# A planned two-stream layer kernel: the order of ScalarE and VectorE by latest times in place of recorded order

## The chip, the cores and the metric

One Trainium2 chip, all 8 cores, no exchange between them. The metric is the device time of the slowest core in microseconds. Engines are named as in the profile: PE is TensorE (matmuls), PEld its weight loads, DVE is VectorE, ACT is ScalarE, POOL is GpSimd and SP is SyncE.

## What is computed

Two layers over x of shape (4, 4096, 1024). Cut to what matters:

```python
for i in range(2):
    h = rmsnorm(x, pre_mix_g)
    proj = h @ w_in + b_in                       # 1024 -> 5120: z, u, v, two gates
    ya = pool_mixer(z) @ w_pa                    # trailing means over 2, 4, 8, 16 positions
    yb = (gelu(u) * (tril(w_s) @ layernorm(gelu(v)) + b_s)) @ w_pb    # in chunks of 128
    x = x + rmsnorm((sigmoid(ga) * ya + sigmoid(gb) * yb) @ w_o, post_mix_g)
    x = x + rmsnorm(square(relu(rmsnorm(x, pre_ffn_g) @ w_ff1)) @ w_ff2, post_ffn_g)
    x = x + rmsnorm(sigmoid(x @ w_ple_gate) * (p[i] @ w_ple_proj), post_ple_g)
```

## The kernel before

Each core owns 2048 positions (and 128 ahead of them as a halo), with the channels on the partitions. The positions are four tiles of 512, worked in two pairs: stream A holds tiles 0 and 2, stream B tiles 1 and 3. Names that end in A or B belong to a stream (XA is its residual, U0A to U56A are its bf16 working tiles, RBA its norm factors). For each pair of tiles and each layer, TensorE runs a group of one to three weight blocks first for A and then for B, so that the weights are loaded once for two tiles (WB has four buffers of one block). Tile 0 has 16 or 32 more columns than the others and so takes two of the eight PSUM banks for each product where the others take one.

The order of a stage, for A and then for B: u (gelu, L740 with tile U3), half of z (L644), v (gelu, L709, its statistics L712), half of the first gate (sigmoid, L740 with U4); then `v_norm` (Ln and Exp, L1080) and the normalised v of both streams (L728, Identity, one for each 128 positions: eight, or nine with the halo); then the rest of z, the gates, the spatial gating product (L788 on TensorE, read by L769 and L772 on VectorE), the pool map, w_pa, w_pb (L844 multiplies by the gate, L847 adds ya), w_o (L859 squares, L863 or L867 scaled copy), ff1 (L931 relu to TMP, L933 product), ff2, and the last stage with the sigmoid gate (L1005 to TMP), the projection (L1015) and their product (L1021), of which ScalarE makes squares (L1024). A sum over channels is a product with ones on TensorE (L500), followed by Ln (L508) and Exp (L511); the residual that follows is eight or twelve operations on VectorE (L891, then L896 or L901), and ScalarE converts its result for the next product (L906, L910).
The pool chain of one chunk: L642 copies the last 16 columns of the tile before into a slot, L644 evicts z behind them, and one to four adds (L659) and L664 follow, through S1 and S2, which both streams share. B has three slots for four chunks.

Nothing is issued as it is written. Each operation is recorded with an engine, a planned duration (for a ScalarE operation from PSUM with a pointer 136 + 0.833 n + 93 ns for n columns, for VectorE from SBUF 185 + 1.042 n) and the operations that it depends on by its tiles. Those dependences are fixed by the recorded order. `Prog._schedule` then simulates the five engines: TensorE, GpSimd and SyncE take their operations in recorded order; ScalarE and VectorE take, whenever they are free, among the operations that are ready the one with the smallest key. The key is `nominal`, the TensorE time recorded ahead of the operation (`late` is 0 everywhere), plus 2500 ns where it needs another table than the one loaded; and such an operation may start only `HOLD_NS` after the last one that used the loaded table. DMAs go through one lane in that simulation: 12 us for the first load of XB (L430), 6.6 us for a weight block. The order that comes out is written to the engines, with a semaphore wait for each dependence.

Of the kernel before, what the change touches and what calls it, by code (L numbers as in the profile page):

```python
# [30 lines left out]
SEM_NS = 90.0  # L31
TABLE_NS = 1300.0
HOLD_NS = 400.0
NS_COL = 0.417

# [8 lines left out]

class Op:
    __slots__ = ("i", "eng", "fns", "ns", "deps", "sem", "inc", "table", "nominal", "late", "tok", "users",
                 "left", "ready", "end")

    def __init__(self, i, eng, fns, ns, deps, sem, inc, table, nominal, late):  # L50
        self.i, self.eng, self.fns, self.ns, self.deps = i, eng, fns, ns, deps
        self.sem, self.inc, self.table, self.nominal, self.late = sem, inc, table, nominal, late
        self.tok = None
        self.users = []
        self.left = 0
        self.ready = 0.0
        self.end = 0.0

class Prog:  # L60
# [6 lines left out]
    def __init__(self):  # L67
        self.ops = []
        self.semh = {}
        self.clock = 0.0  # L70
        self.q = {k: [] for k in self.ENG}

    def add_sem(self, key, handle):
# [29 lines left out]
    def dma(self, eng, sem, fn, ns, reads=(), writes=()):  # L103
        return self._record(eng, [fn], ns, reads, writes, sem, 16)

    def _schedule(self):
        order = {k: [] for k in self.ENG}
        queue = {k: [] for k in self.ENG}
        for o in self.ops:
            o.users = []  # L110
        for o in self.ops:
            o.left = len(o.deps)
            o.ready = 0.0
            for d in o.deps:
                d.users.append(o)
            if o.eng not in self.FREE:
                queue[o.eng].append(o)
        head = {k: 0 for k in self.ENG}
        free = {k: 0.0 for k in self.ENG}
        table, table_end = None, 0.0  # L120
        dma_free = 0.0
        pools = {k: [o for o in self.ops if o.eng == k and o.left == 0] for k in self.FREE}
        left = len(self.ops)
        while left:
            best = None
            for k in self.ENG:
                if k in self.FREE:
                    ps = pools[k]
                    if not ps:
                        continue  # L130
                    def may(o):
                        if o.table is None or o.table == table:
                            return o.ready
                        return max(o.ready, table_end + HOLD_NS)
                    t = max(free[k], min(may(o) for o in ps))
                    pick, key = None, None
                    for o in ps:
                        if may(o) > t:
                            continue
                        x = o.nominal + o.late  # L140
                        if o.table is not None and o.table != table:
                            x += 2500.0
                        if key is None or (x, o.i) < key:
                            pick, key = o, (x, o.i)
                    o = pick
                else:
                    if head[k] >= len(queue[k]):
                        continue
                    o = queue[k][head[k]]
                    if o.left:  # L150
                        continue
                    t = max(free[k], o.ready)
                if best is None or t < best[0]:
                    best = (t, o)
            assert best is not None, "the recorded order cannot run"
            t, o = best
            k = o.eng
            order[k].append(o)
            left -= 1
            if k in self.FREE:  # L160
                pools[k].remove(o)
                dur = o.ns
                if o.table is not None and o.table != table:
                    dur += TABLE_NS
                    table = o.table
                free[k] = o.end = t + dur
                if o.table is not None:
                    table_end = o.end
            elif k == "pe":
                head[k] += 1  # L170
                free[k] = o.end = t + o.ns
            else:
                head[k] += 1
                free[k] = t + 100.0
                dma_free = max(t + 1500.0, dma_free) + o.ns
                o.end = dma_free + 500.0
            for u in o.users:
                u.left -= 1
                u.ready = max(u.ready, o.end + SEM_NS)
                if u.left == 0 and u.eng in self.FREE:  # L180
                    pools[u.eng].append(u)
        self.span = max(o.end for o in self.ops)
        return order

    def build(self, final_eng, final):
# [45 lines left out]
def build_nc():  # L231
# [11 lines left out]
    with ExitStack() as es:  # L243
# [252 lines left out]
        def tail_ones(sq, rsq, cbl):  # L496

            bks = banks(len(cbl))
            for dc in range(8):
                fns = [lambda e, bk=bk, dc=dc, c0=c0, w=w: e.matmul(  # L500
                    PS[:, bk, 0:w], ONEB[:], sq(dc, c0, c0 + w), start=(dc == 0), stop=(dc == 7))
                    for bk, (c0, w) in zip(bks, cbl)]
                P.group(fns, sum(w for _, w in cbl) * NS_COL, reads=[rOne] + rsq(dc), writes=[rPS[bk] for bk in bks])
            return bks
# [771 lines left out]
```

How the kernel before makes its waits and increments, by code:

```python
    def build(self, final_eng, final):  # L185
        order = self._schedule()
        cnt = {}
        for k in self.ENG:
            for o in order[k]:
                cnt[o.sem] = cnt.get(o.sem, 0) + o.inc
                o.tok = (o.sem, cnt[o.sem])
        for k in self.ENG:
            seen = {}
            q = self.q[k]
            for o in order[k]:
                self._waits(k, o.deps, seen, q)
                q.extend(o.fns[:-1])
                s = self.semh[o.sem]
                q.append(lambda e, fn=o.fns[-1], s=s, n=o.inc: fn(e).then_inc(s, n))
            if k == final_eng:
                self._waits(k, final, seen, q)
# [1 line left out]
    def _waits(self, k, deps, seen, q):  # L203
        need = {}
        for d in deps:
            key, val = d.tok
            if key == "pe" and k == "pe":
                continue
            if seen.get(key, 0) >= val:
                continue
            if need.get(key, 0) < val:
                need[key] = val
        for key, val in need.items():
            seen[key] = val
            s = self.semh[key]
            q.append(lambda e, s=s, val=val: e.wait_ge(s, val))
```

## Time and profile before

| | us |
|---|---|
| three runs | 2300.98, 2302.17, 2674.32 (median 2302.17) |
| the profiled execution, its device time | 2302.23 |
| its span, slowest core (core 2) | 2300.7 |
| spans of the eight cores | 2287.4 to 2300.7 |

How to read the rows further on: a busy share says how long an engine ran something; a row of waits says for how long an engine stood still and which operation let it go on (engine, tile, line); a timeline row has start, duration, engine, line, operation, out<-in with shapes and count, and in brackets the idle time before it with its releaser. A row of windows has the bounds and length, then the busy us and instructions of PE, PEld, DVE, ACT and POOL, TensorE's granted clock as a share of full speed, the share of the DMA engines and GB/s.

### The profile page before, as it was taken

To read this page: it belongs to the slowest core of one execution; us is meant where nothing else is said; L and a number is where in the kernel's file an instruction comes from. 1 tells how busy PE (TensorE), PEld (TensorE's weight loads), DVE (VectorE), ACT (ScalarE), POOL (GpSimd) and SP (SyncE) were. 2 spreads that over 40 slices of the span, in tenths; PEclk is the share of its full clock that TensorE was granted. 3 is DMA by queue.
4 is the path that set the end of the run, shared out by engine and by line. 5 is a ranking of instruction groups with operands and counts; after the bars stand their busy time and mean duration, and the time that the engine had idled before them with its cause. 6 is when DMAs were issued, how large, how long until landed. Compare 5 with 4: busy or idle time off the path is not lost.

```text
span 2300.7 us, 30001 instructions; the slowest of 8 cores (2287.4 to 2300.7 us)
## 1 busy us (share of the span) xinstructions
PE 2116.7 (92%) x10640; PEld 1053.2 (46%) x10818; DVE 1019.7 (44%) x1607; ACT 855.7 (37%) x1344; POOL 82.2 (4%) x156
## 2 busy tenths in 40 slices
PE   2989979999798999999979999999989989999995
PEld 1546646666444444444434444444434444444442
DVE  2427553402662755420454565541165375543035
ACT  2353063312645306321454522531165441543134
POOL 0000000000000000000000000000000000000000
PEclk8999989999999999999989999999999999999998
DMA  8332534434343253445484343354343434335331
GB/s 178 56 56 47 92 56 65 75 57 82 72 69 60 47 92 55 68 89 91 84 216 96 65 80 63 66 95 74 55 83 57 76 61 78 69 65 92 62 58 74
DMA packets 36326, 176.83 MB, mean 77 GB/s; under 512 B 3282, under 2 KB 6482, under 8 KB 18770
## 3 DMA queue, kind: packets, MB, share of 16 engines
q0 software_dynamic: 22912, 148.92, 38.1%
q1 hardware_dynamic: 13268, 25.98, 3.5%
q8 instruction: 90, 1.47, 0.3%
q14 instruction: 56, 0.46, 0.1%
HBM read 315.40 MB, written 8.39 MB: 141 GB/s over the span
## 4 chain that ended last, share of the span: by engine, by line
PE 83%; DVE 5%; ACT 5%; issue 5%; DMA 2%; DVEq 0%; SPq 0%; ACTq 0%
PE PS L583 71%; PE PS L701 5%; PE PS L500 3%; DMA XB<-xT 2%; PE PS L805 1%; PE PS L705 1%; DVE XB L896 1%; PE PS L788 1%; ACT U2A L728 1%; DVE XA L901 1%; PE PS L1015 0%; DVE XA L896 0%; ACT U0B L906 0%; ACT L508 0%; ACT TMP L1005 0%
## 5 line engine op out<-in xcount | busy, mean ns | idle before, releaser
L583 PE MATMUL PS<-U0A,WB 128*128 128x512 bf16 (+2 forms) x2907 | 531.7, 341 | 78.5 <-ACT U3A L740 23.5
L583 PE MATMUL PS<-U0B,WB 128*128 128x512 bf16 x2252 | 508.0, 381 | 3.8 <-DVE T L668 1.1
L583 PEld LDWEIGHTS PS<-U0A,WB 128*128 128x128 bf16 x2944 | 291.7, 100 | 302.0 <-issue 88.9
L583 PEld LDWEIGHTS PS<-U0B,WB 128*128 128x128 bf16 x2304 | 225.0, 98 | 268.1 <-issue 7.8
L931 ACT ACTIVATE TMP<-PS 128x512 f32<-128x512 f32 (+1 forms) x256 | 150.3, 597 | 265.4 <-PE PS L583 259.3
L859 ACT ACTIVATE U1A<-PS 128x512 bf16<-128x512 f32 (+1 forms) x64 | 37.5, 605 | 391.2 <-PE PS L583 391.2
L394 POOL DMA_DIRECT2D WB<-wst x144 | 76.3, 531 | 2142.0 <-PE PS L583 1637.4
L583 PE MATMUL PS<-U56B,WB 128*128 128x512 bf16 x504 | 128.1, 406 | 14.5 <-DVE U56B L847 14.1
L583 PE MATMUL PS<-U2B,WB 128*128 128x512 bf16 x498 | 123.7, 395 | 16.1 <-ACT TMP L1005 15.4
L583 PE MATMUL PS<-U2A,WB 128*128 128x512 bf16 (+1 forms) x631 | 123.8, 343 | 10.1 <-ACT TMP L1005 9.7
L583 PE MATMUL PS<-U3A,WB 128*128 128x512 bf16 (+1 forms) x637 | 118.1, 338 | 0.2
L583 PE MATMUL PS<-U3B,WB 128*128 128x512 bf16 x504 | 117.1, 379 | 0.4
L583 PE MATMUL PS<-U56A,WB 128*128 128x512 bf16 (+1 forms) x628 | 116.4, 337 | 0.6
L859 ACT ACTIVATE U1B<-PS 128x512 bf16<-128x512 f32 x64 | 37.4, 598 | 172.1 <-PE PS L583 171.9
L583 PEld LDWEIGHTS PS<-U2A,WB 128*128 128x128 bf16 x640 | 62.7, 99 | 63.9 <-issue 16.3
L583 PEld LDWEIGHTS PS<-U56B,WB 128*128 128x128 bf16 x512 | 52.6, 103 | 84.1 <-issue 31.1
L583 PEld LDWEIGHTS PS<-U2B,WB 128*128 128x128 bf16 x512 | 51.3, 101 | 81.3 <-issue 27.6
L583 PEld LDWEIGHTS PS<-U3A,WB 128*128 128x128 bf16 x640 | 62.7, 98 | 49.2
L583 PEld LDWEIGHTS PS<-U56A,WB 128*128 128x128 bf16 x640 | 62.6, 98 | 49.1
L583 PEld LDWEIGHTS PS<-U3B,WB 128*128 128x128 bf16 x512 | 50.1, 98 | 59.8
L659 DVE TENSOR_TENSOR S<-S 128x525 f32<-128x525 f32 (+5 forms) x96 | 67.4, 702 | 2.9
L769 DVE SCALAR_TENSOR_TENSOR TMP<-PS,CPACK,BF 128x512 f32<-128x512 f32 (+1 forms) x72 | 49.2, 691 | 36.1 <-PE PS L788 32.2
(184 smaller groups left out, 2243.4 us busy)
## 6 DMA issues: line engine op xcount, KB each, us to landing
WB<-wst POOLq DMA_DIRECT2D x136, 1024.0 KB, 8.7
XB<-xT SPq DMA_DIRECT2D x2, 2048.0 KB, 26.5
WB<-wst POOLq DMA_DIRECT2D x8, 512.0 KB, 5.4
outT<-XA SPq DMA_DIRECT2D x16, 256.0 KB, 3.9
outT<-XB SPq DMA_DIRECT2D x16, 256.0 KB, 2.2
XA<-xT SPq DMA_DIRECT2D x4, 528.0 KB, 9.4
U2A<-wsT SPq DMA_DIRECT2D x4, 512.0 KB, 4.0
BF<-bsbc SPq DMA_DIRECT2D x4, 512.0 KB, 4.8
```

Of the source, the lines that this page charges most:

```text
L394: lambda e: e.dma_start(out=WB[:, b, 0:n], in_=wst[l, j, :, 0:n]), 1.6 * n, reads=list(behind), writes=[rW[b]])
L500: fns = [lambda e, bk=bk, dc=dc, c0=c0, w=w: e.matmul(PS[:, bk, 0:w], ONEB[:], sq(dc, c0, c0 + w), start=(dc == 0), stop=(dc == 7)) for bk ...
L583: return lambda e: e.matmul(PS[:, bk, 0:w], WB[:, b, k * kstride + fi * 128: k * kstride + (fi + 1) * 128], rhs(k, c0, c0 + w), start=(k = ...
L659: P.op("dve", dve_ns(COLS - lo, False), lambda e, nxt=nxt, cur=cur, co=co, d=d, lo=lo: e.tensor_tensor(out=nxt[:, lo:COLS], in0=cur[:, lo ...
L701: fns = [lambda e, k=k, lhs=lhs, b=b, bk=bk: e.matmul(PS[:, bk, :], lhs[k], WB[:, b, k * 512:(k + 1) * 512], start=(k == 0), stop=False) f ...
L705: fns.append(lambda e, bk=bk, v0=v0: e.matmul(PS[:, bk, :], ONEB[0:2, :], VB2[0:2, v0:v0 + 512], start=False, stop=True))
L728: P.op("act", act_ns(1024, False, 2), lambda e, c=c, src=src, dst=dst: e.activation(out=dst, in_=src, func=AF.Identity, scale=S.RSTD[:, c ...
L769: P.op("dve", dve_ns(n, True), lambda e: e.scalar_tensor_tensor(out=out, in0=in0, scalar=cv(l, V_LNG, h), in1=in1, op0=ALU.mult, op1=ALU.add),
L788: fns = [lambda e, c=c: e.matmul(PS[:, bk, c * 128:(c + 1) * 128], S.flat(2, c * 2048 + h * 256, 128, BF16), WSB[:, h * 128:(h + 1) * 128] ...
L805: fns.append(lambda e, bk=bk, o0=o0, g=g, cc=cc, c0=c0, w=w: e.matmul(PS[:, bk, 0:w], WB[:, b4, o0:o0 + 128], S.u(1, 2 * g + cc, c0, c0 + ...
L859: P.op("act", act_ns(self.n, True), lambda e: e.activation(out=sv(self.sq(oc, a, b), self.cbs), in_=ps(bks, self.cbs), func=AF.Square), re ...
L931: P.op("act", act_ns(self.n, True), lambda e: e.activation(out=sv(t, self.cbs), in_=ps(bks, self.cbs), func=AF.Relu), reads=rp, writes=[rT ...
```

## The change

The key of ScalarE's and VectorE's operations becomes `due`, a latest time counted backward from the end. The planner simulates forward, computes latest times, and simulates again, eight times in all: the first round uses the old key, the second the times of `_latest` (no engine but TensorE is limited), the later ones those of `_backward`, which runs the same simulation from the end to the start with one operation at a time on each engine and, among those possible, the one that ended last in the forward simulation. The round with the shortest planned span is emitted. Besides, a dependence between two TensorE groups is no longer charged 90 ns, and the 2500 ns have a name.

```diff
--- before.py
+++ after.py
@@ -31,6 +31,8 @@
 SEM_NS = 90.0
 TABLE_NS = 1300.0
 HOLD_NS = 400.0
+SWITCH_NS = 2500.0
+ROUNDS = 8
 NS_COL = 0.417
 
 
@@ -45,7 +47,7 @@
 
 class Op:
     __slots__ = ("i", "eng", "fns", "ns", "deps", "sem", "inc", "table", "nominal", "late", "tok", "users",
-                 "left", "ready", "end")
+                 "left", "ready", "end", "due")
 
     def __init__(self, i, eng, fns, ns, deps, sem, inc, table, nominal, late):
         self.i, self.eng, self.fns, self.ns, self.deps = i, eng, fns, ns, deps
@@ -55,6 +57,7 @@
         self.left = 0
         self.ready = 0.0
         self.end = 0.0
+        self.due = 0.0
 
 
 class Prog:
@@ -68,6 +71,7 @@
         self.ops = []
         self.semh = {}
         self.clock = 0.0
+        self.spans = []
         self.q = {k: [] for k in self.ENG}
 
     def add_sem(self, key, handle):
@@ -103,16 +107,102 @@
     def dma(self, eng, sem, fn, ns, reads=(), writes=()):
         return self._record(eng, [fn], ns, reads, writes, sem, 16)
 
+    def _links(self):
+        for o in self.ops:
+            o.users = []
+        for o in self.ops:
+            for d in o.deps:
+                d.users.append(o)
+
+    def _latest(self):
+
+        last = {k: None for k in self.ENG}
+        for o in reversed(self.ops):
+            t = 0.0
+            for u in o.users:
+                t = min(t, u.due - (0.0 if o.eng == u.eng == "pe" else SEM_NS))
+            if o.eng not in self.FREE:
+                nx = last[o.eng]
+                if nx is not None and o.eng == "pe":
+                    t = min(t, nx.due)
+                last[o.eng] = o
+            o.due = t - (o.ns if o.eng in ("pe",) + self.FREE else o.ns + 2000.0)
+
+    def _backward(self):
+
+        left = {}
+        ready = {}
+        users = {}
+        for o in self.ops:
+            left[o] = len(o.users)
+            ready[o] = 0.0
+        nxt = {k: [o for o in reversed(self.ops) if o.eng == k] for k in self.ENG}
+        head = {k: 0 for k in self.ENG}
+        free = {k: 0.0 for k in self.ENG}
+        pools = {k: [o for o in self.ops if o.eng == k and left[o] == 0] for k in self.FREE}
+        n = len(self.ops)
+        while n:
+            best = None
+            for k in self.ENG:
+                if k in self.FREE:
+                    ps = pools[k]
+                    if not ps:
+                        continue
+                    t = max(free[k], min(ready[o] for o in ps))
+                    o = max((o for o in ps if ready[o] <= t), key=lambda o: (o.end, o.i))
+                else:
+                    if head[k] >= len(nxt[k]):
+                        continue
+                    o = nxt[k][head[k]]
+                    if left[o]:
+                        continue
+                    t = max(free[k], ready[o])
+                if best is None or t < best[0]:
+                    best = (t, o)
+            t, o = best
+            k = o.eng
+            n -= 1
+            if k in self.FREE:
+                pools[k].remove(o)
+                e = free[k] = t + o.ns
+            elif k == "pe":
+                head[k] += 1
+                e = free[k] = t + o.ns
+            else:
+                head[k] += 1
+                free[k] = t + 100.0
+                e = t + o.ns + 2000.0
+            o.due = -e
+            for d in o.deps:
+                left[d] -= 1
+                ready[d] = max(ready[d], e + (0.0 if k == d.eng == "pe" else SEM_NS))
+                if left[d] == 0 and d.eng in self.FREE:
+                    pools[d.eng].append(d)
+
     def _schedule(self):
+        self._links()
+        best = None
+        for o in self.ops:
+            o.due = o.nominal + o.late
+        for n in range(ROUNDS):
+            order = self._forward()
+            if best is None or self.span < best[0]:
+                best = (self.span, order, {o: o.end for o in self.ops})
+            if n % 2 == 0 and n < 2:
+                self._latest()
+            else:
+                self._backward()
+        self.span, order, ends = best
+        for o, e in ends.items():
+            o.end = e
+        return order
+
+    def _forward(self):
         order = {k: [] for k in self.ENG}
         queue = {k: [] for k in self.ENG}
         for o in self.ops:
-            o.users = []
-        for o in self.ops:
             o.left = len(o.deps)
             o.ready = 0.0
-            for d in o.deps:
-                d.users.append(o)
             if o.eng not in self.FREE:
                 queue[o.eng].append(o)
         head = {k: 0 for k in self.ENG}
@@ -121,6 +211,12 @@
         dma_free = 0.0
         pools = {k: [o for o in self.ops if o.eng == k and o.left == 0] for k in self.FREE}
         left = len(self.ops)
+
+        def may(o):
+            if o.table is None or o.table == table:
+                return o.ready
+            return max(o.ready, table_end + HOLD_NS)
+
         while left:
             best = None
             for k in self.ENG:
@@ -128,18 +224,14 @@
                     ps = pools[k]
                     if not ps:
                         continue
-                    def may(o):
-                        if o.table is None or o.table == table:
-                            return o.ready
-                        return max(o.ready, table_end + HOLD_NS)
                     t = max(free[k], min(may(o) for o in ps))
                     pick, key = None, None
                     for o in ps:
                         if may(o) > t:
                             continue
-                        x = o.nominal + o.late
+                        x = o.due
                         if o.table is not None and o.table != table:
-                            x += 2500.0
+                            x += SWITCH_NS
                         if key is None or (x, o.i) < key:
                             pick, key = o, (x, o.i)
                     o = pick
@@ -176,10 +268,11 @@
                 o.end = dma_free + 500.0
             for u in o.users:
                 u.left -= 1
-                u.ready = max(u.ready, o.end + SEM_NS)
+                u.ready = max(u.ready, o.end + (0.0 if k == u.eng == "pe" else SEM_NS))
                 if u.left == 0 and u.eng in self.FREE:
                     pools[u.eng].append(u)
         self.span = max(o.end for o in self.ops)
+        self.spans.append(round(self.span / 1000, 1))
         return order
 
     def build(self, final_eng, final):
```

## Rows read from the trace of the kernel before

**Rows 1.** The page: busy time by engine; the chain that ended last.
```profile
PE 2116.7 (92%) x10640; PEld 1053.2 (46%) x10818; DVE 1019.7 (44%) x1607; ACT 855.7 (37%) x1344; POOL 82.2 (4%) x156
...
PE 83%; DVE 5%; ACT 5%; issue 5%; DMA 2%; DVEq 0%; SPq 0%; ACTq 0%
```

**Rows 2.** TensorE's waits: total us, times, longest us.
```profile
PE PS L583 <- ACT TMP L1005: 25.0, 10, 7.1
PE PS L583 <- ACT U3A L740: 23.5, 3, 20.3
PE PS L583 <- ACT U4B L740: 18.4, 4, 7.8
PE PS L583 <- DVE U56B L847: 14.1, 4, 3.7
PE PS L1015 <- ACT TMP L1005: 13.1, 10, 2.8
PE PS L583 <- DVE U2A L933: 12.8, 4, 9.0
PE PS L583 <- DVE U0A L553: 12.7, 4, 4.3
...
PE PS L788 <- ACT U56B L644: 10.7, 3, 4.6
...
PE PS L1015 <- DVE U3A L1021: 3.2, 1, 3.2
```

**Rows 3.** Windows by engine; before the last two columns the clock.
```profile
365.00:575.00 210.00, 209.27 (x1371) 135.31 (x1383) 54.24 (x72) 52.54 (x87) 9.88 (x18) 1.00 0.46 76
886.00:893.00 7.00, 6.10 (x15) 2.25 (x16) 2.59 (x5) 4.73 (x10) 0.53 (x1) 0.51 0.19 19
...
sum 111.00, PE 77.08 PEld 32.63 DVE 57.64 ACT 72.64 POOL 2.12; mean PE 4.82 PEld 2.04 DVE 3.60 ACT 4.54 POOL 0.13
```

**Rows 4.** Timeline, ScalarE and TensorE, 1283 to 1304: start, us, what.
```profile
1283.25 1.24 ACT L728 ACTIVATE U2A<-U56A,NMR,RSTD 128x1024 bf16<-128x1024 f32 x1 [0.44 <-DVE NMR L1085]
...
1292.43 1.28 ACT L740 ACT_TABLE_LOAD   x1
1293.72 2.42 ACT L740 ACTIVATE U4B<-PS,CPACK 128x512 bf16<-128x512 f32 x4
...
1303.18 0.39 PE L788 MATMUL PS<-WSB,U2A 128*128 128x128 bf16 x4
```

**Rows 5.** Timeline, VectorE and ScalarE, 1296 to 1331 us.
```profile
1296.82 0.71 DVE L659 TENSOR_TENSOR S<-U56A 128x527 f32<-128x527 f32 x1 [5.11 <-ACT U56A L644]
...
1322.29 0.17 DVE L642 COPY U56B<-ZH 128x16 f32<-128x16 f32 x1
...
1323.33 0.69 ACT L740 ACTIVATE U4B<-PS,CPACK 128x512 bf16<-128x512 f32 x1 [1.04 <-PE PS L583]
...
1330.66 0.69 ACT L644 ACTIVATE U56B<-PS,CPACK 128x512 f32<-128x512 f32 x1 [2.96 <-DVE U56B L642]
```

**Rows 6.** Timeline, VectorE and TensorE, 876 to 899 us.
```profile
876.05 2.35 DVE L891 TENSOR_TENSOR U2A<-U2A,RBA 128x1024 f32<-128x1024 f32 x2
...
885.14 1.28 DVE L844 TENSOR_TENSOR U56B<-PS,U56B 128x512 bf16<-128x512 f32 x2
886.33 0.75 DVE L847 TENSOR_TENSOR U56B<-U56B,U4B 128x512 bf16<-128x512 bf16 x2
...
886.90 11.74 PE L583 MATMUL PS<-U56B,WB 128*128 128x512 bf16 x39 [3.46 <-DVE U56B L847]
```

**Rows 7.** Timeline, VectorE, 1162 to 1175 us.
```profile
1162.17 2.36 DVE L891 TENSOR_TENSOR U3A<-U3A,RBA 128x1024 f32<-128x1024 f32 x2 [3.57 <-ACT RBA L511]
...
1172.02 2.69 DVE L1021 TENSOR_TENSOR U3B<-PS,TMP 128x512 f32<-128x512 f32 x4
```

**Rows 8.** The chain and ScalarE's timeline at the start.
```profile
4.50 43.83 DMA XB<-xT
...
48.41 4.27 ACT L542 ACTIVATE U1B<-XB 128x512 bf16<-128x512 f32 x8 [27.70 <-DMA XB<-xT]
```

## The prediction

> **What bounds the kernel now.** I read the page first. TensorE is busy 92% of the span, VectorE 44%, ScalarE 37% [rows 1]. The chain that ended last is 83% TensorE, with 5% each of VectorE and ScalarE [rows 1]: those ten per cent are seams, places where TensorE stands still for an operation of one of the two. The change leaves TensorE's instructions and their order alone, so it can touch only that standing still and what follows from it. The profiled execution took 2302.2 us, its span is 2300.7, and the median of the three runs is 2302.2 too, so I sum against 2302.2.
>
> Second view, the list of TensorE's waits over the span [rows 2]. Its 16 rows add up to 159 us; the nine that carry the terms below are shown. Third, the timelines around the waits, to see what the releasing engine was doing in the meantime. If it was busy with something that nobody needed yet, another order removes the wait; if it waited itself, none does. Fourth, windows with the granted clock: between seams it is 1.00 (365 to 575 us), at a seam, after TensorE had stood still, 0.51 [rows 3], that is the lower of its two levels (1.2 for 2.4 GHz). So a wait costs more than its own length.
>
> **The change, part by part.** No instruction is added or removed. The orders of TensorE, GpSimd and SyncE stay as recorded. What changes is the key by which the planner picks among ready operations of ScalarE and VectorE. Before: the TensorE work recorded ahead of it. After: the latest time at which it can run. Eight rounds are tried and the one with the shortest planned span is emitted. The rounds cost nothing on the chip; the 90 ns no longer charged between TensorE groups only moves planned times. The 2500 ns for a table switch are the same number. So the whole effect is in five places.
>
> (a) Gate evictions behind the normalised v. ScalarE runs eight L728 of 1.23 us (nine of them in the first tile pair), then a table load, then the four L740 of U4B, whose PSUM banks TensorE wants; TensorE stops meanwhile [rows 4]. The first matmul that reads their output (L788) starts only at 1303.2 [rows 4], some 11 us after the last L728, so nothing needed them that early. By latest time L740 goes first, even with the 2.5 us surcharge. Waits 18.4 us in 4 places [rows 2]. I take 17.4; 1 us stays, for an L728 that still goes first in the tiles with twice the banks.
>
> (b) Pool chain. B's fourth eviction L644 waits for a copy (L642), and that for the end of an earlier pool chain on VectorE; L788 waits for the bank [rows 5]. The chains of A and B share S1 and S2, so they can't change places; only the gate products (L769, L772) between them can move, and A's first L644 can start earlier once (a) is gone. 10.7 us [rows 2]; between 0 (the chain itself is the bound) and all of it I take 8, because VectorE stood idle for 5.1 us at this stage's start, waiting for an L644 that stood behind (a) [rows 4, 5].
>
> (c) Residuals before evictions. VectorE runs eight residual operations of A, 9.1 us from 876.1 on, and only then L844 and L847 of B, which TensorE waits for until 886.9. The residual's result is first read by ff1 of A, after the 11.7 us of matmuls that start there, at 898.6, or about 895 once the wait of 3.5 is gone [rows 6]. Putting L844 and L847 (2.0 us) ahead delays the residual only to the 887.1 at which VectorE is through with both now [rows 6]. That is 14.1 us (4 times L847). The same at ff1: the residual of B, then A's L933, 12.8 us in 4 places, of which 9.0 in the first tile pair [rows 2]; I take 12.0. Together 26.1. What is late next: the residual of B, which four L933 of some 0.65 us delay by 2.6 us. Before ff1 of B reads it TensorE still has the rest of ff1 of A to do, more than 5 us. It holds.
>
> (d) The last stage of a layer. VectorE runs A's whole residual (9.9 us, 1162.2 to 1172.0) before four products L1021 of B; these free the three TMP slots, so the fourth L1005 and TensorE wait, 7.1 us [rows 7]. In A's part of that stage it is B's residual, with ScalarE's eight L910 beside it. These waits are 25.0, 13.1 and 3.2 us, 41.3 together [rows 2]. What no order removes: the first L1005 needs its table load, which I put at 1 us of wait in each of the eight half-stages (the load is 1.28 [rows 4]), and where layer 1 follows within the same tiles the residual is itself needed for the next squares, another 3. I leave 11 and take 30.
>
> Sum of (a) to (d): 17.4 + 8 + 26.1 + 30 = 81.5 us.
>
> (e) The clock. In the 16 windows around the lower level that belong to those waits TensorE was busy 77.1 us [rows 3]. Matmuls there take twice as long, so half of it, 38.5, is lost; the windows are rounded outward, which leaves about 34, and some short waits stay. I take 30.
>
> What stays. The start: ScalarE is at eight squares of B (L542) that wait for XB until 48.4 us, and the L740 that TensorE wants stand behind them, 20.3 us [rows 2, 8]. One would hope for these, but the planner charges XB 12 us while it takes 43.8 [rows 8] and the first weights only come after it in its one DMA lane, so by its clock the squares are ready long before any L740 and an idle engine takes what is ready, whatever the key. 0 us; if I am wrong, 20 less. The norm latency at each layer's start (table load, L508, L511, L553: 12.7 us in 4 places [rows 2]) is a chain with nothing in between. The tail after the last matmul is a chain as well. SyncE is a strict queue: if A's XA comes later, so do its stores and the reload of XA behind them, which the next post-mix reads some 200 us on. GpSimd's weight loads wait for TensorE alone.
>
> (f) What it adds. A finer interleaving means that each engine, which runs strictly in order, more often stands at an operation that is a little late while another is ready. One instance is there already: the L740 at 1323.3 stands ahead of the L644 whose copy L642 was done at 1322.5 [rows 5]. The planner knows no clock level, and its durations are rounded. The bounds: 0, and 0.8 us at each of 60 or so evictions near seams, 50 us. I take one such wait in each of 16 stages, 13 us, and 7 for four falls of the clock: 20.
>
> A rule of the Trainium skill speaks against the change. ScalarE: Activation LUTs, "What ACT_TABLE_LOAD costs" and the rules for authors: a switch of table set costs 2.66 us in all, a load and a drain, and one should do all of one set before switching. The trace shows the load (1.28 us) and the next activation 0.02 us after it [rows 4], with no further gap. By the page's figure an extra pair of switches would be an estimated 5.3 us, by the rows 2.6.
>
> **Sum.** 2302.2 - 81.5 - 30 + 20 = 2210.7, so 2211 us, 4.0% less. Its own range: all 97.3 us of the five groups and 34 of clock with nothing added gives 2171; half the waits and half the clock, nothing added, 2246.
>
> **Rivals.**
> Half of it (2246 to 2290, say 2262): each residual goes behind the evictions and then is late itself, and clock falls stay because the waits are split rather than gone. For: at the seam of layer 0 to 1 the residual, 9.9 us [rows 7], and eight products must fit into one half-stage of some 20 us with the squares behind them. Against: VectorE is 44% busy in all [rows 1], and in (c) the residual ends no later than now. Worked out: half of 81.5 and of 30 is 56, and three quarters of (f) still come on top, some 16: 2302 - 56 + 16 = 2262.
> No change (2300): the planned span of the first round, which uses the old key, wins, or the new order moves work only where TensorE doesn't wait. For: the shortest plan may be that one. Against: the planner knows these durations (0.66 us for an L740, 1.25 for an L891), so its own plan must contain these waits and see them go.
> Slower (2350): table switches. Latest times alternate between gelu, sigmoid and ln in the v stage and the last stage; a pair is 2.57 us [rows 4] in front of an eviction, plus 1.7 for a clock fall (3.4 us of matmuls at half speed). It decides where it eats the 91.5 us that the sum gains: 91.5 / 4.3 is 22 exposed pairs; 2350 would be 33 pairs, four for each of the eight tile-layers, every one exposed. Against: the surcharge and the hold are unchanged. The page's rule points this way.
>
> **Chances.** Forecast 0.72, half of it 0.15, no change 0.09, slower 0.04. Since 2% is about what a measurement of this kernel can tell from no change, faster by over 2% (below 2256) is 0.72 + 0.08 + a little for a plan that gains even more = 0.81; within 2% 0.16; slower by over 2% 0.03. For 8 in 10 I widen the forecast's own range upward: 2168 to 2270.
>
> **What would show it.** TensorE's matmul count unchanged and its busy time about 30 us less than 2116.7 [rows 1]. In the waits: L847, L933 and U4B L740 nearly gone, TMP L1005 near 10 us, U3A L740 still 20 at the start, L553 still 12. In the timeline at each seam L844 ahead of L891, L1021 ahead of L901. Granted clock at the seams 1.00. I am wrong if ScalarE's table loads rise by tens, if L906 or L542 appears among TensorE's releasers with several us, or if the order is as before.

## The result and the profile after

The changed kernel takes 2175.8 us (median of four runs, 2175.6 to 2177.3); the ratio to before is 0.9455, with an interval of 0.9432 to 0.9478. The forecast was 2211, with a range of its own from 2171 to 2246. In some executions the cores of one die show a lower mean granted clock and longer spans than those of the other (0.979 and 2214.2 us beside 0.987 and 2198.4 in one run below), so the medians here leave out the executions that this lengthened most, and "on die 1" stands for the median span of cores 4 to 7. The profiled execution took 2177.3 us, its span is 2175.4, so 125.3 us of span are gone, where the sum had 91.5.

In the changed kernel every line that the prediction names stands 93 further down: L583 is now L676, L553 L646, L644 L737, L728 L821, L740 L833, L788 L881, L844 L937, L847 L940, L891 L984, L933 L1026, L1005 L1098, L1015 L1108, L1021 L1114. First the page, which answers to [rows 1]:

```profile
PE 2075.9 (95%) x10640; PEld 1043.8 (48%) x10818; DVE 1016.7 (47%) x1607; ACT 848.1 (39%) x1344; POOL 82.1 (4%) x156
...
PE 92%; DMA 3%; ACT 2%; issue 2%; DVE 1%; SPq 0%; DVEq 0%; ACTq 0%; POOLq 0%
```

TensorE has the same 10640 matmuls in the records and is busy 40.8 us less. VectorE and ScalarE have the same work within 1%. The chain that ended last is 92% TensorE where it was 83%: the two shares of 5% for VectorE and ScalarE have shrunk to 1% and 2%.

TensorE's waits after, which answer to [rows 2]:

```profile
PE PS L676 <- ACT U3A L833: 22.6, 2, 20.3
PE PS L676 <- DVE U0A L646: 13.6, 4, 4.6
...
PE PS L676 <- DMA WB<-wst: 10.4, 1, 10.4
PE PS L1108 <- ACT TMP L1098: 7.9, 8, 1.7
...
PE PS L676 <- ACT U1A L1037: 1.7, 1, 1.7
PE PS L676 <- ACT U56A L737: 1.3, 2, 1.0
...
PE PS L676 <- ACT U4B L833: 0.3, 1, 0.3
...
PE PS L881 <- ACT U56B L737: 0.2, 1, 0.2
```

All its rows add up to 74.4 us, where they were 159.3. L847, L933 and L1021 are gone from the list, U4B fell from 18.4 to 0.3, L644 from 10.7 to 0.2 and TMP from 38.1 to 7.9: eight waits of 0.8 to 1.7 us. What was not to move has not moved: the start (U3A, 20.3 in one wait), the norm (L646, 13.6). The wait of 10.4 us for WB at the start stands where the one for U0A L572 (9.1) stood.

Three seams show how. The residual of A and the last evictions behind w_pb, on VectorE (as in [rows 6], there at 876 us):

```profile
829.74 1.22 DVE L984 TENSOR_TENSOR U2A<-U2A,RBA 128x1024 f32<-128x1024 f32 x1
830.88 0.69 DVE L937 TENSOR_TENSOR U56B<-PS,U56B 128x512 bf16<-128x512 f32 x1
831.48 1.22 DVE L989 TENSOR_TENSOR XA<-XA,U2A 128x1024 f32<-128x1024 f32 x1
...
832.95 0.69 DVE L937 TENSOR_TENSOR U56B<-PS,U56B 128x512 bf16<-128x512 f32 x1
...
841.79 1.22 DVE L989 TENSOR_TENSOR XA<-XA,U3A 128x1024 f32<-128x1024 f32 x1
```

The gate products L937 (before: L844) now stand between single residual operations. The residual ends only at 843.0, and TensorE begins with its converted chunks (U0A) at 845.6 without a pause. The last stage of a layer (as in [rows 7]):

```profile
1101.95 2.36 DVE L984 TENSOR_TENSOR U3A<-U3A,RBA 128x1024 f32<-128x1024 f32 x2 [0.16 <-ACT RBA L604]
1104.60 2.48 DVE L1114 TENSOR_TENSOR U3B<-PS,TMP 128x512 f32<-128x512 f32 x4 [0.29 <-ACT TMP L1098]
1107.00 2.35 DVE L984 TENSOR_TENSOR U4A<-U4A,RBA 128x1024 f32<-128x1024 f32 x2
1109.27 1.44 DVE L1114 TENSOR_TENSOR U4B<-PS,TMP 128x512 f32<-128x512 f32 x2
```

Four products L1114 come after the first two L984 instead of after twelve residual operations. And ScalarE behind the layer norm of v (the stage of [rows 4], one layer on):

```profile
1743.88 0.69 ACT L833 ACTIVATE U4B<-PS,CPACK 128x512 bf16<-128x512 f32 x1
1744.44 1.25 ACT L821 ACTIVATE U2B<-U56B,NMR,RSTD 128x1024 bf16<-128x1024 f32 x1
1745.58 1.27 ACT L737 ACTIVATE U56A<-PS,CPACK 128x512 f32<-128x512 f32 x2
1747.07 0.69 ACT L833 ACTIVATE U4A<-PS,CPACK 128x512 bf16<-128x512 f32 x1 [0.21 <-PE PS L676]
```

The evictions U4B (L833) and U56A (L737) alternate with the normalised v (L821), where eight of these had run in one piece.

Windows around one of the short waits that stayed and around one norm wait (columns as in [rows 3]):

```profile
1103.00:1107.00 4.00, 3.07 (x14) 1.17 (x14) 3.71 (x6) 3.99 (x7) 0.53 (x1) 1.00 1.06 253
596.00:604.00 8.00, 5.69 (x21) 2.48 (x23) 5.52 (x8) 2.72 (x6) 0.00 (x0) 0.79 1.01 150
```

In the first lies a wait of 0.82 us for TMP, and the clock is 1.00 throughout; in the second lies one of 4.63 us, and the mean is 0.79. In windows of 4 us over the whole span the lower level shows only at the start (40 to 72 us), at three norm waits (from 596, 1116 and 1640 us) and at the end (from 2164 us). Before, it showed at these places too, and at the seams besides.

### The profile page after: what moved, and what is told of

The parts are those of the page before. It is cut to its first block, busy times and chain, and to the rows that moved or that the text cites. A ratio compares the mean times of both kernels' runs of the same rounds, so it can differ in the third digit from the quotient of the medians.

```text
span 2175.4 us, 30026 instructions; the slowest of 8 cores (2170.3 to 2175.4 us)
## 1 busy us (share of the span) xinstructions
PE 2075.9 (95%) x10640; PEld 1043.8 (48%) x10818; DVE 1016.7 (47%) x1607; ACT 848.1 (39%) x1344; POOL 82.1 (4%) x156
## 4 chain that ended last, share of the span: by engine, by line
PE 92%; DMA 3%; ACT 2%; issue 2%; DVE 1%; SPq 0%; DVEq 0%; ACTq 0%; POOLq 0%
PE PS L676 80%; PE PS L794 5%; PE PS L593 3%; DMA XB<-xT 2%; PE PS L798 1%; PE PS L898 1%; PE PS L1108 1%; DMA WB<-wst 1%; PE PS L881 1%; ACT L1098 0%; PE PS L565 0%; ACT TMP L1098 0%; DVE U0A L906 0%; DVE XB L994 0%; ACT U1B L635 0%
## 5 line engine op out<-in xcount | busy, mean ns | idle before, releaser
L676 PE MATMUL PS<-U0A,WB 128*128 128x512 bf16 (+2 forms) x2907 | 525.5, 338 | 51.8 <-ACT U3A L833 22.6
L676 PE MATMUL PS<-U0B,WB 128*128 128x512 bf16 x2252 | 503.1, 379 | 3.1 <-ACT U56B L737 0.4
L676 PEld LDWEIGHTS PS<-U0A,WB 128*128 128x128 bf16 x2944 | 289.6, 99 | 271.4 <-issue 60.7
L676 PEld LDWEIGHTS PS<-U0B,WB 128*128 128x128 bf16 x2304 | 224.0, 98 | 264.2 <-issue 1.4
L676 PE MATMUL PS<-U2A,WB 128*128 128x512 bf16 (+1 forms) x631 | 120.5, 337 | 0.5
L676 PE MATMUL PS<-U3A,WB 128*128 128x512 bf16 (+1 forms) x637 | 118.0, 338 | 0.2
L676 PE MATMUL PS<-U2B,WB 128*128 128x512 bf16 x498 | 116.8, 379 | 0.9
L676 PE MATMUL PS<-U3B,WB 128*128 128x512 bf16 x504 | 117.1, 379 | 0.4
L676 PE MATMUL PS<-U56A,WB 128*128 128x512 bf16 (+1 forms) x628 | 116.4, 337 | 0.6
L676 PE MATMUL PS<-U56B,WB 128*128 128x512 bf16 x504 | 116.0, 379 | 0.4
L676 PEld LDWEIGHTS PS<-U2A,WB 128*128 128x128 bf16 x640 | 62.3, 98 | 51.0 <-issue 1.7
L676 PEld LDWEIGHTS PS<-U3A,WB 128*128 128x128 bf16 x640 | 62.6, 98 | 49.3
L676 PEld LDWEIGHTS PS<-U56A,WB 128*128 128x128 bf16 x640 | 62.6, 98 | 49.0
L676 PEld LDWEIGHTS PS<-U56B,WB 128*128 128x128 bf16 x512 | 50.1, 98 | 60.4
L676 PEld LDWEIGHTS PS<-U3B,WB 128*128 128x128 bf16 x512 | 50.1, 98 | 59.8
L676 PEld LDWEIGHTS PS<-U2B,WB 128*128 128x128 bf16 x512 | 49.8, 98 | 59.9 <-issue 1.4
## 6 DMA issues: line engine op xcount, KB each, us to landing
WB<-wst POOLq DMA_DIRECT2D x136, 1024.0 KB, 10.8
```

The lines of the kernel that those rows point to most:

```text
L676: return lambda e: e.matmul(PS[:, bk, 0:w], WB[:, b, k * kstride + fi * 128: k * kstride + (fi + 1) * 128], rhs(k, c0, c0 + w), start=(k = ...
```

## The experiments

All are edits of the changed kernel. The first batch:

**The old key, one round.**
```diff
-ROUNDS = 8
+ROUNDS = 1
```

> One round only, so the old key (recorded TensorE time) decides, without the 90 ns between TensorE groups. Theory (the key is the whole effect): the order is nearly the one of before, the ten seam waits with L847, L933, U4B L740, L644 and TMP L1005 are back at some 97 us, TensorE's busy time at 2117, time 2300, within 0.5% of before. Rival (the planned TensorE times were wrong by the 90 ns, and that alone let the planner misplace operations): the time falls by 20 us or more.

2302.0 us, ratio 0.9993 (0.9962 to 1.0024), with 157.5 us of waits. The 90 ns and the named constant do nothing that can be measured; the key is the change.

**One backward pass.**
```diff
-ROUNDS = 8
+ROUNDS = 2
```

> Two rounds: the second, whose key is the plain latest time counted back through the users with no engine but TensorE limited, is emitted. The planner puts it 2.2 us above the eight rounds in its own span and 99 us below the old key. Theory (most of the gain is earliest deadline first, of any reasonable deadlines): 2178, within 0.3% of the change. Rival (the backward simulation with one operation at a time on each engine is what places the residuals): 2200 or more.

2178.8 us, 0.9449 (0.9381 to 0.9518), 73.2 us of waits. The plain latest times, in which only TensorE is limited, have the whole gain within 3 us. Whether the backward simulation and the rounds that use it are worth these 3 us can't be told, since the two versions did not run side by side.

**Latest times on VectorE alone.**
```diff
-                        x = o.due
+                        x = o.due if o.eng == "dve" else o.nominal + o.late
```

> Latest times on VectorE alone, ScalarE by the old key. Theory (each wait belongs to the engine whose queue was in the wrong order): the waits for U4B L740 stay at 18 us (ScalarE's eight L728), those for L847 and L933 go, TMP L1005 falls to about 15; with the clock 2215 to 2225. Rival (an order with one engine on old terms starves the other): above 2250.

2227.3 us, 0.9661 (0.9591 to 0.9731). Its waits:

```profile
PE PS L676 <- ACT U4B L833: 18.2, 4, 7.8
...
PE PS L881 <- ACT U56B L737: 9.3, 3, 4.6
...
PE PS L676 <- ACT TMP L1098: 8.0, 5, 2.5
```

The time is 2 us above the theory's range. U4B stays at 18.2, as the theory had it. Of the waits for TMP 8.0 us stay at L676 and 8.2 at L1108 (the change has 7.9 there), near the 15 expected. L881's 9.3 I had not named: the pool chain is not freed from VectorE's side.

**Latest times on ScalarE alone** (the same line with "act"):

> Latest times on ScalarE alone, VectorE by the old key. Theory: U4B L740 goes (18 us) and most of L788's wait for L644 (10), L847 and L933 stay at 27 and TMP L1005 at 30 or more; with the clock 2255 to 2265. The two single parts (x3 and x4) then save 80 + 42, about the 126 of the whole. Rival: the parts overlap or need each other, and their sum is off the whole by more than 20 us.

2261.5 us, 0.9809 (0.9749 to 0.9868). Its waits:

```profile
PE PS L676 <- ACT TMP L1098: 24.9, 6, 5.7
...
PE PS L676 <- DVE U56B L940: 14.1, 4, 3.7
...
PE PS L676 <- DVE U2A L1026: 11.2, 3, 8.8
```

L881 is down to 1.5 us here, so the pool chain is freed almost wholly from ScalarE's side. The parts save 75 and 41 us, together 116 of the 126: additive to 10 us. The row for TMP at L676 is where both queues hold something back: 25.0 before [rows 2], 8.0 in the first run, 24.9 in the second, none with both.

The next batch does single places by hand, under the old key. The times over all cores are given, and those on die 1, where the kernel before had 2291.1 us on the same chip (five executions, 2288.3 to 2294.7). The change did not run beside them; in its own two batches it had 2172.6 and 2172.2 on die 1, so its gain there is taken as some 119 us.

**(a) alone.**
```diff
-ROUNDS = 8
+ROUNDS = 1
...
-                        reads=rs + [rRSTD, rNMR], writes=rd)
+                        reads=rs + [rRSTD, rNMR], writes=rd, late=12000.0)
```

> The old key everywhere, with 12 us added to the key of the normalised v (the eight ScalarE operations ahead of the U4B evictions) and nothing else. Theory (place (a) is a matter of these operations alone): the wait for U4B L740-type evictions (18.3 us) falls below 3, L788's wait for L644 falls as well because the pool chain starts earlier, and with the clock the time is 2270 to 2282. Rival (VectorE's pool chain takes over as the bound and gives the gain back): 2290 or more.

2284.3 us over all cores, ratio 0.9929 (0.991 to 0.9949), and 2272.3 on die 1: 16 or 19 us for the 18.3 of waits. The theory's 2270 to 2282 holds on die 1 only. U4B is out of the list; 4.5 us stay at U56A L737, and L881 is still at 9.1, so its second half fell: (b) doesn't come with (a).

**Products first on VectorE.**
```diff
-                        reads=rp + [rTMP[tb]], writes=[S.rU[u][c]])
+                        reads=rp + [rTMP[tb]], writes=[S.rU[u][c]], late=-20000.0)
```
and the same `late` on L844, L847 and L1021.

> The old key, except that VectorE's products that TensorE or a TMP slot waits for (gate product and add behind w_pb, the ff1 product, the product of the last stage) come ahead of everything else. Theory: places (c) and the VectorE part of (d) go, 27 + 25 us of waits and half of the clock loss: 2225 to 2235, near the run with latest times on VectorE alone (2227). Rival (the residuals, pushed behind every product, become late for the next product of TensorE): waits for U0A, U0B or U2B of over 10 us appear and the time is above 2250.

2245.1 us over all cores, 0.9763 (0.9746 to 0.978), and 2232.2 on die 1, 55 or 59 us less than before; the theory's 2225 to 2235 holds on die 1 only. L847 is gone and L933 down to 0.2, and the only new row of its list above 1 us is L1037 with 1.8. The residuals were not urgent at these seams. TMP keeps 21.3 us in two rows, and L881 its 10.7, so neither (a) alone nor VectorE's products alone free the pool chain.

**Both rules, and evictions first on ScalarE** for ff1 and the last stage:

> The two hand rules of the last two runs together, plus evictions first on ScalarE for ff1 and the last stage; still no latest times. Theory (what matters is which few operations go behind the evictions, not the exact times): 2195 to 2205, three quarters or more of the gain, the pool chain (L644) and a few us at the residuals missing. Rival: the backward times do something that no fixed rule does, and the time stays above 2220.

2217.2 us over all cores, 0.9637 (0.9617 to 0.9658), and 2199.7 on die 1. With a `late` at seven places the time on die 1 falls by 91 us of some 119, three quarters of the gain; over all cores it falls by 83, and there the time is above the theory's range. L881 keeps 9.3 us, and 4.1 stay at U56A L737.

**No surcharge for a table**, the forecast's slower rival:
```diff
-HOLD_NS = 400.0
-SWITCH_NS = 2500.0
+HOLD_NS = 0.0
+SWITCH_NS = 0.0
```

> The change with SWITCH_NS and HOLD_NS at 0, so that a table is switched whenever the latest times say so. It is the forecast's slower rival. Theory: more table loads than 49, each 1.28 us with the next activation right behind, half of them exposed: 2185 to 2200. Rival (the page's figure: a load and a drain, 2.66 us in all): the gap between the operation before a load and the one after it is 2.7 us and the time is 2205 or more. Third: the number of loads does not rise and the time stays at 2177.

2199.9 us over all cores, 0.9564 (0.9545 to 0.9583), and 2188.3 on die 1. Groups of table loads in this run, and after it the one of the change:

```profile
L833 ACT ACT_TABLE_LOAD x21 | 26.9, 1283 | 32.3 <-PE PS L676 32.1
...
L1176 ACT ACT_TABLE_LOAD x4 | 5.1, 1283 | 0.1
```

```profile
L833 ACT ACT_TABLE_LOAD x16 | 20.5, 1283 | 32.1 <-PE PS L676 32.0
```

59 loads in place of 49, each 1.28 us, and on die 1 the time is some 16 us above the change's in its own batches. TensorE's list has new waits of 9.2 us for L737 at L881 and of 3.4 for L821. The run changes the order as well as the number of loads, so how much of the 16 us is the ten loads is not shown. The four at L1176 have 0.1 us of idle time ahead of them, all together. So a load is 1.28 us here, and no drain shows beside it. The Trainium skill (ScalarE: Activation LUTs, "What ACT_TABLE_LOAD costs") has 2.66 us for a switch, a load and a drain. This trace doesn't show the second part. The Trainium skill (the same page, "Rules for kernel authors") also advises to do all of one set before switching. The run agrees with that: without surcharge and hold the time is longer. For the change this was no danger, since it has the 49 loads of before.

The third batch, with the change itself beside it:

> The change itself, beside the three above on the same chip, as their measure: 2174 to 2179.

2176.3 us, 0.9455 (0.9436 to 0.9473), 71.1 us of waits. Its profile and that of the first run have records of all 10818 matmuls, so (e) can be read there a second time: TensorE is busy 2087.2 us beside 2127.6, again 40.4 less.

**Skewed durations.**
```diff
+SLOW = {"act": 0.6, "dve": 1.5}
...
+        ns *= SLOW.get(eng, 1.0)
         op = Op(len(self.ops), eng, fns, ns, deps, sem, inc, table, self.clock, late)
```

> The change with skewed planned durations: ScalarE's times 0.6, VectorE's times 1.5. Theory (the order by latest times is set by who reads what and when, and survives skewed durations; that is why the forecast's 20 us for operations that come a little late were not found): 2180 to 2195. Rival (the exact durations make the interleaving fit, and skewed ones bring back waits of about 1 us at most evictions near seams): 2210 or more.

My theory fell: 2253.1 us (median of four executions, 2251.4 to 2273.3; 0.9788, 0.9764 to 0.9812), and 2246 to 2250 on cores 0 to 3 of the profiled one. VectorE at the start of core 2:

```profile
40.88 1.22 DVE L584 CAST U3B<-U2B 2x2048 bf16<-2x2048 f32 x1 [13.91 <-DMA U2B<-bvrow]
42.02 0.33 DVE L663 SCALAR_TENSOR_TENSOR U2A<-U56A,CPACK,U3A 128x128 bf16<-128x128 f32 x1
...
43.42 0.17 DVE L667 COPY U0A<-U2A 128x128 bf16<-128x128 bf16 x1
```

The plan has the cast L584 ahead of the last L663 and the copy L667, as if bvrow had landed by then. VectorE stands at the cast for 13.9 us, and TensorE waits 23.8 us for the copy. It looks like a part of the loss, but it isn't: B's first u products, here and in the change's repeat, begin at

```profile
81.50 20.67 PE L678 MATMUL PS<-U0B,WB 128*128 128x512 bf16 x94
```

```profile
83.83 20.88 PE L676 MATMUL PS<-U0B,WB 128*128 128x512 bf16 x96
```

The change loses the same time to its own waits at the start (21.2 us for U3A and 8.5 for U0A in the repeat). The loss comes later. 26 us are waits for U56B L739 (L644 before), 21.0 of them at L883, the product that stands behind the pool chain, where the change's repeat has 0.6 in its two rows. Another 13.0 us are twelve waits for ScalarE's conversions of the residual (U2B L1005 6.9, U0A L1001 6.1), which the change does not have. (Lines stand two further down in the runs with scaled durations.)

Was it the ratio or the error? Two more runs:

> The change with the planned durations of ScalarE and VectorE both multiplied by 1.3. The skewed run (0.6 and 1.5) took 2264 where I had expected 2180 to 2195. Theory A (the planner must know which of the two engines is the slower one; a common factor keeps the order): 2178 to 2195. Theory B (any error of 30% makes it see a bound on VectorE that isn't there, and the pool-chain waits for L644 come back as in the skewed run): 2210 to 2240, with L644 waits of 10 us or more.

2222.3 us in the profiled execution and 2222.8 in a second, beside 2299.5 of before (no interval from two). There are 27.1 us of waits for U56B L739, as theory B had it. The copy of the halo, L667, has a wait of 32.4 us, but B's first u products begin at 85.5 us, only 1.7 later than in the change's repeat.

> The change with planned durations 0.8 for ScalarE and 1.2 for VectorE, half the skew of the run before in each. Theory A (the loss grows with the skew): 2190 to 2210. Theory B (one misplaced operation at the start, VectorE's cast that waits for a DMA, and the pool chain carry the loss, and either is there or not): below 2182, or above 2210 with the 24 us wait for the halo copy U0A back.

2219.5 and 2219.2, ratio 0.965 (0.963 to 0.9671). Neither theory: the time is above 2210, but without the wait for the halo copy. The cast is in its right place and the start as in the change; 23.8 us of waits for U56B L739 remain. What happens there, in ScalarE's and VectorE's and TensorE's timelines of this run:

```profile
1806.05 0.69 ACT L835 ACTIVATE U4B<-PS,CPACK 128x512 bf16<-128x512 f32 x1 [1.04 <-PE PS L678]
1807.78 0.69 ACT L835 ACTIVATE U4B<-PS,CPACK 128x512 bf16<-128x512 f32 x1 [1.04 <-PE PS L678]
1808.36 1.26 ACT L739 ACTIVATE U56B<-PS,CPACK 128x512 f32<-128x512 f32 x2
```

```profile
1804.58 0.25 DVE L737 COPY U56B<-ZH 128x16 f32<-128x16 f32 x2
1809.14 0.71 DVE L754 TENSOR_TENSOR S<-U56B 128x527 f32<-128x527 f32 x1 [4.32 <-ACT U56B L739]
```

```profile
1818.37 0.59 PE L883 MATMUL PS<-WSB,U2B 128*128 128x128 bf16 x4 [6.72 <-ACT U56B L739]
```

VectorE has both copies for B's next z done at 1804.8 and the evictions could run, but ScalarE's next in line are two gate evictions that wait for TensorE; it comes to L739 at 1808.4, VectorE idles 4.3 us, and TensorE in the end 6.7. The change has it the other way round:

```profile
1766.93 1.26 ACT L737 ACTIVATE U56B<-PS,CPACK 128x512 f32<-128x512 f32 x2 [4.41 <-DVE U56B L735]
1768.68 0.69 ACT L833 ACTIVATE U4B<-PS,CPACK 128x512 bf16<-128x512 f32 x1 [0.49 <-PE PS L676]
```

L737 at 1766.9, and the gate eviction at 1768.7 without loss. That is the forecast's (f), an operation in order behind one that isn't ready, with durations 20% off: against the change's repeat the list is 29.7 us longer (100.8 for 71.1) and TensorE busy 13.8 us more (2101.0 for 2087.2), together 43.5 of the 43.9 by which the span is longer.

**The start, ScalarE's order.** The planner adds a time to the landing of that one load:
```diff
-                o.end = dma_free + 500.0
+                o.end = dma_free + 500.0 + o.late
...
-xT[:, :, c0:c0 + n]), 12000.0, writes=S.rX)
+xT[:, :, c0:c0 + n]), 12000.0, writes=S.rX, late=32000.0 if t == 1 else 0.0)
```

> The change, with the planner told that the first load of XB lands 32 us later, so that ScalarE's first two U3A evictions come before the eight squares of B. Theory: the 20 us wait of TensorE for the U3A eviction shrinks to a few us, but TensorE's next but one group is the sum of those squares, so a wait of 8 to 14 us appears there instead; only the matmuls between the two are gained: 3 to 8 us less than the change (2176). Rival A (the whole 20 us go): 2158. Rival B (the wait just moves): within 2 us of the change.

2168.1 us, 0.9419 (0.9402 to 0.9435), 8.1 less than the change's repeat, at the upper end of the theory's 3 to 8. In its waits:

```profile
PE PS L593 <- ACT U1B L635: 7.2, 1, 7.2
PE PS L676 <- ACT U3A L833: 3.7, 2, 2.2
```

Of the 23.4 us at U3A in the repeat 3.7 are left, but 7.2 have come up at the sum of B's squares. Against the change's repeat the list is 10.5 us shorter (60.6 for 71.1), and TensorE is busy 1.0 us more (2088.2 for 2087.2).

**The start, both orders.**
```diff
-                ia += [(4 if prev is None else 0, B.premix_squares), (6 if prev is None else 9, B.premix_norm),
-                       (10, lambda: sgu_setup2(l))]
+                ia += [(4 if prev is None else 0, B.premix_squares), (14 if prev is None else 9, B.premix_norm),
+                       (10 if prev is not None else 99, lambda: sgu_setup2(l))]
```

> As the last one, and for the first pair of tiles the sum of B's squares on TensorE is recorded eight groups later and the preparation of the spatial bias after the first three blocks of A, so that TensorE has A's u and z to do while XB lands. Theory: of the 20 us of wait 15 or more go, and TensorE leaves the lower clock level earlier: 2155 to 2163. Rival (the weight blocks of A land too late, since they share the DMA engines with XB): a wait for WB of 5 us or more in the first 60 us and 2168 or more.

2158.7 us, 0.9377 (0.936 to 0.9393): 17.6 us less than the change's repeat, and the fastest version here. TensorE from its first product on:

```profile
29.60 5.12 PE L676 MATMUL PS<-U0A,WB 128*128 128x264 bf16 x27
36.94 18.17 PE L676 MATMUL PS<-U0A,WB 128*128 128x264 bf16 x144 [2.22 <-ACT U3A L833]
54.95 1.94 PE L593 MATMUL PS<-U1B,ONEB 128*128 128x512 bf16 x8
...
64.20 11.13 PE L676 MATMUL PS<-U0B,WB 128*128 128x512 bf16 x43 [3.74 <-DVE U0B L646]
```

It works through A's u and z from 36.9 to 55.0 without a pause and waits 3.7 us for the norm of B. The list is down to 54.0 us.

## Why the prediction was right and where not

The direction and the places were right; the size was 34 us short: 91.5 us forecast, 125.3 less span measured. 2175.8 us lies inside the forecast's own range, 5 us from the lower end, which is all waits and all clock with nothing added. By its own terms:

| term | forecast | measured |
|---|---|---|
| (a) U4B | 17.4 | 18.1 |
| (b) pool chain | 8 | 10.5 |
| (c) residuals behind w_pb and in ff1 | 26.1 | 26.9 |
| (d) last stage | 30 | 33.4 |
| (e) clock | 30 | 40.8 |
| (f) what it adds | 20 | 4.0 |

The measured values are the differences of the wait lists; (e) is TensorE's busy time with the same count of matmuls; (f) is what is in the rest of the list now and wasn't (66.0 for 62.0: L1037 1.7, L737 1.7 in three waits, 1.3 at the first weights, 0.9 at the norm, 0.8 in small ones, less 2.4 in rows that fell). 88.9 + 40.8 - 4.0 is 125.7, the span fell by 125.3.

**(f) is the step that failed**, with 16 of the 34 us. I reasoned that finer interleaving must bring ordered waits, and priced 16 at 0.8 us and four falls of the clock at 7 us. There are four new waits for an eviction or a square (L1037, L737), 3.4 us in all, and no fall of the clock at a place that had none before. The scaled runs speak for this reason: in the planner's durations the interleaving is tight, and it holds on the chip because they are right (0.66 us planned for an L740 that takes 0.69, 1.25 for an L891 of 1.22). With both durations 30% too long, or 20% off in opposite directions, the same key loses 46 and 43 of its 126 us. I had taken the one late operation I found in the order of before [rows 5] as a sample of the new order; but that order's key had nothing to do with when an eviction is wanted.

**(e)** is the second mis-sized term, 10.8 us short. I took 8.5 off the 38.5 for rounding and for falls that stay, and none of the falls in its 16 windows stayed: the short waits that remain in the last stage, six of 0.82 us, one of 1.25 and one of 1.68, leave the clock at 1.00. The measured 40.8 is even above the 38.5. A part of that lies at norm waits, which the 16 windows leave out: by the granted clock the lower level lasted some 6.8 us at 628 to 640 and at 1736 to 1744 us before, and 3.4 us at 596 to 604 and at 1640 to 1648 after. The mean clock of core 2 went from 0.966 to 0.990, so the time at the lower level fell from about 156 to 44 us (twice the missing share of the span).

**(b) and (d)** together were 5.9 short. In (b) I left room for the chain as the bound, and it isn't: only 0.2 us stay once both queues go by latest times. ScalarE's queue does most of it alone (1.5 us stay), VectorE's does not (9.3). In (d) 3 us were set aside for the seam from layer 0 to 1, where the residual is needed; L984 and L1114 fit in there as everywhere.

**What stays** was right in all three places: the start at 20.3, the norm at 13.6, the table loads at 49. The start stays because of the planned landing, as the step says: with that put right the same key wins 8 us, and with TensorE's order changed too 18.

**The rivals.** No change falls with the first run: the old key alone gives 2302, so the emitted plan isn't that of the first round. Half of it falls with the list of waits, where 88.9 of 97.3 us are gone. The slower one has a real mechanism: the run with ten more loads takes some 16 us longer, at most 3.2 a pair where the rival had 4.3. But the change has none of them: 49 loads before and after.

## What to carry to other kernels

In a planned order the key matters more than the search: one backward pass of latest times over the users gave all but 3 us of 126. Evictions and products that free a bank or a slot are urgent and residuals are not: seven places put right by hand gave three quarters. Look in the timeline for the engine that a wait names: if it was busy with work that is read much later, that wait can be had, and with it about half as much again in clock (88.9 and 40.8 us here). Then measure the planner's durations and landings, since they are what makes a fine interleaving hold in order: 20% of error in opposite directions took a third of the gain back, and one load charged 12 us for 44 held 8 us more (18 with TensorE's own order changed as well).

## What the runs showed of the hardware

The short waits of TensorE for TMP that remain (0.82 us six times, 1.25, 1.68) lie in windows with the granted clock at 1.00, and so do the one of 1.73 us for U1A L1037 at 321.8 us and, in the kernel before, the one of 1.24 us at 913.7 us; I had taken something off the clock term for such waits. A table load took 1.28 us in each of 59 cases, with 0.1 us of idle time ahead of four of them together.
